# One-hot operands of an expert-gate scatter: four tokens interleaved, or one run of 128 per token

## The reference, cut to what matters

```
e1, e2 = ...            # per token, 8 heads x 16 picks = 128 picks: two key numbers, each 0..127
gates  = softmax(best)  # per token, 128 gates
a   = einsum("td,thkd->thk", xb, u[e1 * 128 + e2])
act = gates * gelu(a)
y   = einsum("thk,thkd->td", act, v[e1 * 128 + e2])
```

## Time and profile before

| | |
|---|---|
| median of 3 runs | 3619.91 us (3618.64 to 3622.04) |
| profiled execution | 3621.95 us, its span 3620.1 us |
| PE busy | 3302.0 us, 91% of the span |
| DVE busy | 2658.1 us, 73% |
| ACT busy | 1100.8 us, 30% |
| hot matmuls L1583 | 1152, 144.1 us busy |
| hot builds L1212, L1213, L1216 | 240 instructions, 33.0 + 32.9 + 91.2 us busy |
| the stage with the hot loop | about 1898.8 to 2457 us of the span |

### The profile page before, as it was taken

The page is one execution under the profiler, slowest core; times in us unless marked ns, Lnnn a source line. Parts: engine busy times, 40 slices in busy tenths (PEclk is TensorE's granted clock), DMA queues, the critical chain, the costliest instruction groups (busy, mean ns, idle before and its releaser), DMA issues.

```text
span 3620.1 us, 46724 instructions
## 1 busy us (share of the span) xinstructions
PE 3302.0 (91%) x17301; PEld 3012.7 (83%) x17301; DVE 2658.1 (73%) x3062; ACT 1100.8 (30%) x1015; POOL 847.9 (23%) x456
## 2 busy tenths in 40 slices
PE   1598877879979899999989999999999998999999
PEld 0386655547758799999989999999999998999999
DVE  6858996875473389888877777775777777677777
ACT  2122113433122244444333322222333332333332
POOL 0205671000020002222101222220343333333333
PEclk7699889989979999999999999999999999999999
DMA  8572111214524447777657777776999999999997
GB/s 353 212 295 74 70 64 55 96 71 189 197 102 160 154 145 268 269 286 268 232 195 266 278 282 284 288 273 253 352 349 343 349 345 330 343 342 350 343 349 290
DMA packets 241084, 883.47 MB, mean 244 GB/s; under 512 B 17680, under 2 KB 132496, under 8 KB 169744
## 3 DMA queue, kind: packets, MB, share of 16 engines
q1 hardware_dynamic: 161552, 545.82, 40.9%
q0 software_dynamic: 55296, 268.46, 19.9%
q10 hardware_dynamic: 24192, 68.64, 5.1%
HBM read 824.13 MB, written 58.72 MB: 244 GB/s over the span
## 4 chain that ended last, share of the span: by engine, by line
PE 60%; DVE 17%; issue 13%; DMA 6%; ACT 4%; DVEq 1%; SPq 0%; POOL 0%; ACTq 0%; PEldq 0%; POOLq 0%
PE bank L1608 9%; PE bank L1610 9%; PE bank L1609 9%; PE bank L1307 8%; PE bank L1309 7%; PE bank L1308 7%; DVE u_row L1138 3%; ACT w_hi L448 3%; DMA w_raw<-wwq 2%; PE bank L1583 2%; DMA ada_w<-wada 2%; PE bank L1499 2%; PE bank L1500 2%; PE bank L1501 2%; DVE hot L1216 1%
## 5 line engine op out<-in xcount | busy, mean ns | idle before, releaser
L779 DVE TENSOR_TENSOR w_lo<-w_raw,w_hi 128x2048 fp32r<-128x2048 f32 (+1 forms) x309 | 701.4, 2270 | 774.2 <-ACT w_hi L448 763.4
L1307 PE MATMUL bank<-act_hi,w_hi 128*128 128x384 f32 (+1 forms) x2840 | 1033.6, 364 | 201.7 <-POOL act_lo L406 106.0
L448 ACT ACTIVATE w_hi<-w_raw 128x2048 fp32r<-128x2048 f32 (+1 forms) x327 | 621.9, 1902 | 1559.5 <-PE bank L1309 835.8
L1308 PE MATMUL bank<-act_lo,w_hi 128*128 128x384 f32 (+1 forms) x2840 | 1016.7, 358 | 0.0
L1309 PE MATMUL bank<-act_hi,w_lo 128*128 128x384 f32 (+1 forms) x2840 | 1015.7, 358 | 0.0
L1307 PEld LDWEIGHTS bank<-act_hi,w_hi 128*128 128x128 f32 x2840 | 549.0, 193 | 272.0 <-issue 164.9
L1608 PE MATMUL bank<-wt_hi,w_hi 128*128 128x384 f32 x2048 | 688.9, 336 | 17.5 <-DVEq L1268 9.0
L1609 PE MATMUL bank<-wt_lo,w_hi 128*128 128x384 f32 x2048 | 686.8, 335 | 0.0
L1610 PE MATMUL bank<-wt_hi,w_lo 128*128 128x384 f32 x2048 | 686.6, 335 | 0.0
L1309 PEld LDWEIGHTS bank<-act_hi,w_lo 128*128 128x128 f32 x2840 | 548.3, 193 | 35.7
L1308 PEld LDWEIGHTS bank<-act_lo,w_hi 128*128 128x128 f32 x2840 | 549.8, 194 | 30.6 <-issue 0.2
(11 more groups left out here) (235 smaller groups left out, 2853.3 us busy)
## 6 DMA issues: line engine op xcount, KB each, us to landing
w_raw<-u SPq DMA_DIRECT2D x128, 1024.0 KB, 7.8
w_raw<-v SPq DMA_DIRECT2D x128, 1024.0 KB, 5.1
ada_w<-wada SPq DMA_DIRECT2D x80, 1024.0 KB, 5.1
gelu_l<-gelu_scratch SPq DMA_DIRECT2D x64, 768.0 KB, 6.4
gate_l<-gate_scratch SPq DMA_DIRECT2D x64, 768.0 KB, 9.4
w_raw<-win SPq DMA_DIRECT2D x27, 1024.0 KB, 6.8
gelu_scratch<-gelu_s ACTq DMA_DIRECT2D x128, 192.0 KB, 2.5
gate_scratch<-g_chunk ACTq DMA_DIRECT2D x8, 3072.0 KB, 12.4
```

The source lines that it names most:

```text
L448: act.activation(w_hi[n0 % 2][:, 0:width], w_raw[n0 % 2][:, 0:width], ACT.Copy).then_inc(hi_done, 1)
L779: dve.tensor_tensor(w_lo[s][:, 0:width], w_raw[s][:, 0:width], w_hi[s][:, 0:width].bitcast(F32), ALU.subtract).then_inc(lo_done, 1)
L1307: pe.matmul(out, wh, hi_t(k), start=(k == 0), stop=False)
L1308: pe.matmul(out, wh, lo_t(k), start=False, stop=False)
```

## The change

The hot tiles become [8 tokens, 128 key numbers] for each half: each token's one-hot row is one contiguous run of 128 bf16 elements. PE reads it with a step of one. The constant is 128 elements long and is read once for every token; the token's value (`e1_c`, `e2_c`, `gate_c`) is read 128 times in a row, so that the innermost dimension of this input has a step of zero. Count of instructions, elements per instruction (1024 per partition), types, waits and their order stay as they are.

```diff
-        hot2 = at("hot2", 176, [P, 2, 2, P, 4], BF16)
-        hot1 = [at(f"hot1{j}", 180 + 4 * j, [P, 2, 2, P, 4], BF16) for j in range(3)]
+        hot2 = at("hot2", 176, [P, 2, 8, P], BF16)
+        hot1 = [at(f"hot1{j}", 180 + 4 * j, [P, 2, 8, P], BF16) for j in range(3)]
...
-        iota4 = at("iota4", 209, [P, P, 4], BF16)
...
+        iota_c = at("iota_c", 211.5, [P, P], BF16)
...
-            T_.mark(dve.tensor_copy(iota4[:], iota_f[:].unsqueeze(2).broadcast_to([P, P, 4])))
+            T_.mark(dve.tensor_copy(iota_c[:], iota_f[:]))
...
-            iotas = iota4[:].unsqueeze(1).broadcast_to([P, 2, P, 4])
+            iotas = iota_c[:].unsqueeze(1).broadcast_to([P, 8, P])
...
             def of_tokens(row, tok):
-                return row[:, tok].rearrange("p (g t) -> p g t", t=4).unsqueeze(2).broadcast_to([P, 2, P, 4])
+                return row[:, tok].unsqueeze(2).broadcast_to([P, 8, P])
...
-                                last = pe.matmul(o, hot2[:, u, g, :, q], hot1[j][:, u, g, :, q], start=(j == 0), stop=(j == 2))
+                                last = pe.matmul(o, hot2[:, u, 4 * g + q, :], hot1[j][:, u, 4 * g + q, :], start=(j == 0), stop=(j == 2))
```

More of the change, by code:

```diff
@@ L1212, in _ @@
                     one = T_.mark(dve.tensor_tensor(hot1[2][:, u], iotas, of_tokens(e1_c, tok), ALU.is_equal))
-                    dve.tensor_tensor(hot2[:, u], iotas, of_tokens(e2_c, tok), ALU.is_equal)
+                    dve.tensor_tensor(hot2[:, u], iotas,
+                                      of_tokens(e2_c, tok), ALU.is_equal)
                     T_.after(one)
```

## The result

The changed kernel takes 3691.35 us in the median (3689.64 to 3693.19), against 3620.97 us for the kernel before in the same comparison. The ratio is 1.0194, with a 95% interval of 1.0182 to 1.0206: slower, by 70 us, where 3697 us was forecast. Its span in the profiled execution is 3690.2 us, 70.1 more than before.

What follows compares the result with a forecast made beforehand. The prediction took the chain through VectorE's builds behind two dots, for which PE waits, as the bound. Slower builds +64, faster hot matmuls -12 and clock drops +25 gave +77 us, 3697 us, range 3640 to 3735.

Steps and rivals of the forecast that it cites:

- Chain: Hot loop: builds behind two dots (long) end last and PE waits, so each added microsecond lengthens the kernel, 23 times.
- about zero at worst: Builds behind one dot (short): cover before PE needs them shrinks from 2.4 to about 1.3 us, or about zero.
- Rate of the build: VectorE's five build instructions fall to single rate, 687 to 1225 ns each: 2.69 us a build, +64 us in all.
- The hot block: PE's 24 hot matmuls per build get faster with contiguous reads: 0 to -35 us, taken as -12 us.
- I lean to the old rate, and take a third: PE's hot block: estimate between 115 and 52 ns a matmul, giving 2.25 us instead of 2.77, -12 us.
- The bound of 52 ns: PE's hot matmuls: the fastest start-to-start time at 128 columns, worked out from the 384- and 512-column times.
- The clock: PE's longer waits, 3.4 to 3.9 us, cause 16 more drops to half clock at 1.55 us each: +25 us.
- PE gains all: Rival: hot matmuls gain fully, -35 us, and the clock stays up despite a 3.9 us gap; 3649 us, chance 0.1.
- The sum: Whole kernel: 64 - 12 + 25 = +77 us, giving 3697 us.
- half clock through whole jobs: Sign of a wrong prediction: 8 us of PE work at 0.50 would cost 4 us a turn, 3790 us.
- the rate holds: Rival: VectorE's builds still take a repeated element at two per cycle; 3608 us (3620 to 3585), chance 0.09.
- DVE's idle time hides it: Rival: VectorE's 150 us of idle time absorbs the slower builds' 129 us; 3608 us, chance 0.04.

Runs made afterwards that it cites:

- e4_filled: The changed kernel with 24 more 384-column matmuls in each half 0, into an unused bank, where PE waits for the long build; 3640.79 us, ratio 1.0058.
- e5: The changed kernel with the dots moved behind the builds, so that a build directly follows lo on VectorE; 3595.05 us, ratio 0.9932.
- e6: The kernel before with the dots moved behind the builds on VectorE; 3599.19 us, ratio 0.9943.
- e7: The changed kernel with each token's value stored twice as neighbours and the dots moved behind the builds on VectorE; 3525.69 us, ratio 0.9738.
- e1_pairs: The changed kernel with each token's value stored twice, as a pair of neighbours repeated 64 times; 3601.77 us, ratio 0.9948.
- e3_dve_runs: The changed kernel with its matmuls reading with a step of four (tokens mixed), VectorE's half of the change alone; 3707.08 us, ratio 1.0238.
- e2_pe_runs: The kernel before with its matmuls reading runs of 128 (tokens mixed), TensorE's half of the change alone; 3601.91 us, ratio 0.9946.

## Why the prediction was right

Its steps, with what the runs gave for each:

- **Chain.** A turn is the offset from the job's last start to PE's start on the long build, plus the hot block, plus the job. The first was forecast at 14.9 us with slow builds and measured 14.86. The short builds came in time, as forecast, but only with the clock's help: at full clock (e4_filled) TensorE waits some 0.2 us for them, the "about zero at worst" of the prediction. The same sum gives 24.42 us for e4_filled, and the same offsets gave the turns of e5 (22.39), e6 (22.40) and e7 (19.48), where one engine's own work is the bound.
- **Rate of the build.** 2.69 us a build forecast, 5 x (1.216 - 0.687) = 2.65 measured. e1_pairs shows the cause. The Trainium skill's sentence (Vector Engine (DVE) Microarchitecture Reference, section 5.1) that one repeated element takes the double rate away from a two-source instruction held for a run of 128 repeats as well.
- **The hot block.** Here the step "I lean to the old rate, and take a third" mis-sized the rate: at full clock it fell to 55 ns, the far bound, and not to the 94 that -12 us stood for. (The bound of 52 ns was itself read loosely: it is what 128 more columns add. The straight line through the two widths leaves 20 ns besides and would give 72, which the measured 55 does not bear out.) The old row was at 115 through its own step of four, not through the weight load. The Trainium skill's 81 ns (TensorE: Matmul & The Clock Gate, section "Back-to-back issue gap") is too high as well: the trace of the changed kernel has 55. Yet the term came out near: from e3_dve_runs to the changed kernel it is 3691 - 3707 = -16 us. The block that counts runs at half clock, where a run of 128 takes 104 ns and not 55, against the stepped 114. So the block itself gives only 0.27 us of the 0.66 between these two kernels' turns; the other 0.39 is half clock that the job behind it is spared. That the term came near is luck: its reason was another.
- **The clock.** 16 more falls at 1.55 us were forecast. The clock falls in every turn, behind a wait that is 4.8 us and not 3.4 to 3.9, since the faster hot block behind the short build brings PE sooner to each wait (0.70 + 2.64 + 1.44 = 4.78; the rival "PE gains all" kept 3.9 us, where its own full gain makes 4.9). It costs 2.19 us a turn against 23.50 - 23.24 = 0.26 before. That is 23 x 1.93 = 44 us in place of 25.
- **The sum.** Per turn: 2.65 for the build, 1.33 - 2.77 = -1.44 for a block at full clock, 1.93 for the clock, together 3.14, against 3.11 measured. Over 23 turns these are +61, -33 and +44 us, where the prediction had +64, -12 and +25. At full clock the block gained 21 us more than forecast and the clock lost 19 more, and the two nearly cancel. They are not independent: of the clock's 2.19 us a turn 1.16 are the block itself (2.49 in place of 1.33), so the clock takes most of the block's gain back. The mechanism was right in each step, but two terms were mis-sized, and that the total came within 7 us is in part luck. The prediction's figure for half clock through whole jobs, 3790, also counts the clock twice: 4 us a turn in place of the 25 us already in the sum gives 3764.

The rival "the rate holds" fell with the rows of the builds in the profile after, and "DVE's idle time hides it" with the waits. That rival had named its own condition, builds that do not stand behind the dots. Under it, in e5_order_after, VectorE's idle time does take up the builds, and the change costs nothing against the old layout; but the idle time is then used up, and builds at double rate are worth 69 us more.

Alone, in the old order, the two halves are worth -19 us (e2_pe_runs) and +86 us (e3_dve_runs). The best version found is e7_order_pairs, 3525.69 us, 2.6% below the kernel before: runs of 128 for PE, pairs for VectorE, and the builds ahead of the dots. The first two together, without the new order, gave 19 us (e1_pairs), and the new order alone 20 (e6_order_before); all three give 94.

## What to carry to other kernels

An engine that is busy 73% of the time can still set the end, if what the bound engine waits for stands behind other work in its queue; look for which instruction ends last, and try its place in the queue as well as its rate: from the changed kernel, the double rate alone gave 90 us, the place alone 96, and both together 166. A broadcast in bf16 keeps VectorE's double rate if the repeated thing is a pair of neighbours, so store it twice (684 ns here, against 1215 with a single element repeated). A wait that grows on TensorE costs more than its length when the clock falls behind it: count it with the half-speed stretch.

## What the runs showed of the hardware that was not expected

- A bf16 moving operand with a step of four elements (8 bytes) runs at 112 to 115 ns for 128 columns, at 1.2 GHz as at 2.4 GHz; with a step of two or one it is 55 to 57 ns at 2.4 GHz and 102 to 104 at 1.2. So the limit with a step of four does not follow the array's clock.
- 55 ns from start to start at 128 columns includes a weight load for every matmul, whose own record is 98 ns long; the loads are wholly hidden.
- More work on TensorE made a kernel 51 us faster (e4_filled), and the clock's 2.19 us a turn are the whole of it.
- Behind waits of one length, 4.77 us in the changed kernel, the clock came back after different times, and the turns took 25.7 to 27.2 us. Behind waits of 2.1 us (e1_pairs, e2_pe_runs) it fell in 15 turns of 22.
